# One hybrid decoder layer on one core: the place of the last norm's sums among the steps of a group

## What is computed

```python
proj = n1 @ w_in                                 # (320 x 2048) @ (2048 x ...)
xbc_c = silu(causal_dwconv(xbc, xbc0, ssm_conv_w, ssm_conv_b))     # B, C and x, 4 taps
xs, Bm, Cm = split_last(xbc_c, ...)
y, h_new = ssd_scan(xs_h, dt, A, Bm, Cm, ssm0)   # 8 groups of 8 heads
y = y + ssm_d[:, None] * xs_h
y = y * silu(z)
yg = y.reshape(b, L, 8, 512)                     # one norm for each group
yg = yg * rsqrt(mean(yg * yg, axis=-1) + EPS)
branch_a = (yg * ssm_norm) @ w_ssm_out
```

## Time and profile before

| | us |
|---|---|
| median of three runs | 2808.53 |
| lowest and highest | 2807.86, 2808.56 |
| the profiled execution's own time | 2808.5 |
| its span | 2806.8 |
| TensorE busy in the span | 2783.4 (99%) |
| VectorE busy | 1782.3 (63%) |
| ScalarE busy | 1165.9 (42%) |
| mean granted TensorE clock, share of full | 0.996 |

### The profile page before, as it was taken

One profiled execution on the slowest core, in us unless ns is written; L12 is line 12 of the kernel. 1 busy time (PEld: TensorE's weight loads), 2 busy tenths in 40 slices (PEclk: granted clock), 3 DMA queues, 4 the chain that ended last, 5 costly groups with the idle time before them and its releaser, 6 DMA issues.

```text
span 2806.8 us, 53359 instructions
## 1 busy us (share of the span) xinstructions
PE 2783.4 (99%) x19380; PEld 2753.6 (98%) x19380; DVE 1782.3 (63%) x2247; ACT 1165.9 (42%) x1712; POOL 294.5 (10%) x457
## 2 busy tenths in 40 slices
PE   8999999999999999999999999999999999999998
PEld 7999999999999999999999999999999999999998
DVE  8888878887888655545454556555555555555564
ACT  5654454544544333333333336333333333333453
POOL 2222221222222100000000001000000000000100
PEclk9999999999999999999999999999999999999999
DMA  8887887887878665555555554555555555555553
GB/s 227 223 213 193 213 229 187 199 219 197 215 194 210 187 178 149 155 145 147 150 150 150 149 149 133 166 150 146 149 149 149 149 149 149 149 149 149 151 166 113
DMA packets 910210, 477.18 MB, mean 170 GB/s; under 512 B 167802, under 2 KB 903746, under 8 KB 909778
## 3 DMA queue, kind: packets, MB, share of 16 engines
q1 hardware_dynamic: 833345, 433.15, 57.3%
q10 hardware_dynamic: 76080, 40.03, 5.2%
q0 software_dynamic: 672, 2.66, 0.2%
HBM read 449.95 MB, written 25.79 MB: 169 GB/s over the span
## 4 chain that ended last, share of the span: by engine, by line
PE 97%; DVE 1%; ACT 0%; issue 0%; DMA 0%; SPq 0%; ACTq 0%; DVEq 0%
PE ps L1842 31%; PE ps L1843 31%; PE ps L1844 31%; PE ps L2098 1%; PE ps L1950 1%; PE ps L2114 1%; PE ps L2016 0%; PE ps L2006 0%; PE ps L2007 0%; PE ps L2233 0%; PE ps L2240 0%; PE ps L2244 0%; DMA xrow<-in_x_sample 0%; PE ps L2105 0%; PE ps L2218 0%
## 5 line engine op out<-in xcount | busy, mean ns | idle before, releaser
L1842 PE MATMUL ps<-n_hi,whi 128*128 128x320 f32 x4144 | 1285.2, 310 | 0.8 <-DVE chunk L1573 0.6
L1844 PE MATMUL ps<-n_hi,wlo 128*128 128x320 f32 x4144 | 1280.6, 309 | 0.0
L1843 PE MATMUL ps<-n_lo,whi 128*128 128x320 f32 x4144 | 1280.5, 309 | 0.0
L1176 DVE TENSOR_TENSOR wlo<-raw,whi 128x1024 fp32r<-128x1024 f32 x746 | 922.2, 1248 | 462.7 <-ACT whi L782 461.9
L782 ACT ACTIVATE whi<-raw 128x1024 fp32r<-128x1024 f32 x746 | 783.3, 1057 | 833.6 <-PE ps L1844 722.1
L1842 PEld LDWEIGHTS ps<-n_hi,whi 128*128 128x128 f32 x4144 | 778.0, 188 | 3.6 <-DVE chunk L1573 0.9
L1843 PEld LDWEIGHTS ps<-n_lo,whi 128*128 128x128 f32 x4144 | 777.9, 188 | 1.3
L1844 PEld LDWEIGHTS ps<-n_hi,wlo 128*128 128x128 f32 x4144 | 777.8, 188 | 0.0
L1842 PE MATMUL ps<-c_hi,whi 128*128 128x320 f32 x1728 | 535.1, 310 | 0.5 <-DVE c_lo L1299 0.5
L1844 PE MATMUL ps<-c_hi,wlo 128*128 128x320 f32 x1728 | 533.9, 309 | 0.0
L1843 PE MATMUL ps<-c_lo,whi 128*128 128x320 f32 x1728 | 533.9, 309 | 0.0
(11 more groups left out here) (309 smaller groups left out, 1752.6 us busy)
## 6 DMA issues: line engine op xcount, KB each, us to landing
raw<-in_w_in SPq DMA_DIRECT2D x322, 512.0 KB, 4.6
raw<-in_w_ffn_gate SPq DMA_DIRECT2D x88, 512.0 KB, 4.6
raw<-in_w_ffn_up SPq DMA_DIRECT2D x88, 512.0 KB, 5.0
raw<-in_w_ffn_down SPq DMA_DIRECT2D x88, 512.0 KB, 4.0
raw<-in_w_ssm_out SPq DMA_DIRECT2D x64, 512.0 KB, 6.0
hs<-in_state_ssm ACTq DMA_DIRECT2D x32, 512.0 KB, 5.9
hq<-in_state_ssm SPq DMA_DIRECT2D x512, 32.0 KB, 3.3
out_ssm_sample<-hs ACTq DMA_DIRECT2D x32, 512.0 KB, 3.6
```

Of the source, the lines that this page charges most:

```text
L1176: tt(wlo[slot][:], raw[slot][:], whi[slot][:].bitcast(F32), SUB).then_inc(lo_split, 1)
L1842: mm(out, w_h, x_h, start=first, stop=False)
L1843: mm(out, w_h, x_l, start=False, stop=False)
L1844: return mm(out, w_l, x_h, start=False, stop=last)
```

## The change

In the list for groups 1 to 7 `norm` moves from behind the second unit to behind the fourth, directly ahead of `bc`, and `lows` moves from behind the third unit to behind `bc`. Nothing is added and nothing is removed; group 0, the short-convolution segment and all other segments keep their lists.

```diff
-        head = (x(0, 1) + [("norm", 0)] + x(2) + [("lows", 0)] + x(3) + [("bc", 0)] + x(4)
+        head = (x(0, 1) + x(2) + x(3) + [("norm", 0), ("bc", 0), ("lows", 0)] + x(4)
                 + OUT8[:1] + [("flip", 0)] + OUT8[1:3] + [("old", 0)] + OUT8[3:5] + [("decay", 0), ("clamp", 0)]
                 + OUT8[5:6] + [("exps", 0)] + OUT8[6:] + [("mask", 0)] + x(5))
```

## The result

| | before | after |
|---|---|---|
| median, us | 2808.55 | 2847.8 |
| lowest and highest | 2807.86, 2808.73 | 2847.5, 2849.72 |
| span of the profiled execution | 2806.8 | 2845.9 |
| mean granted TensorE clock | 0.996 | 0.991 |

The ratio is 1.0143, with a 95% interval of 1.0131 to 1.0155: the change makes the kernel 39.3 us slower. The forecast was 2833.8, and its range ended at 2846.0. The sign and the place were right, but the time lies 1.8 us outside the range.

The account below looks back on a forecast made before the run. TensorE was taken to bound the loop, with no idle time to absorb a wait. (3.52 + 0.1) x 7 = 25.3 us on 2808.5 gave 2833.8 us, +0.9%, with a range of 2829 to 2846.

Parts of the forecast that it names:

- What bounds the kernel: In the loop TensorE is busy 112.00 of 112.00 us a round, so any new wait adds to the time, seven-fold.
- Part 1: TensorE's own work at the norm's sums: same work in another order, gain taken as 0, at most 2.8 us.
- Part 2: First out step: the third c_lo tile comes at T + 12.53, TensorE is ready at T + 9.18; 3.52 us lost a round.
- Part 3: Third and sixth out steps: VectorE's later additions may delay TensorE by 0 to 1 us a round; 0.1 taken.
- The rival of the clock: TensorE's clock falls in the new gap: another 16 us, 2850 in all rounds, 2836 to 2848 in some; chance 0.15.
- The rival of a covered wait: c_lo arrives before the fifth unit ends, 2808.5 to 2811.7 us; bc behind lows would leave 0.45 us a round; chance 0.06.

Follow-up runs that it names:

- the kernel with other banks: Changed kernel with lows ahead of bc, the first out step writing banks 2 and 3, its b_stacked and cbm_ready waits one step later: 2832.3 us.
- the kernel with a gap of 3.8 us: Changed kernel with lows ahead of bc behind the fourth unit: 2850.6 us, ratio 1.0154 to the kernel before.

## Why the prediction was right and wrong, point by point

- **What bounds the kernel, and that a wait has no slack to go into.** Right. 7 waits, and no other engine's change shows in the loop. Only moving `lows` gave 0.9999, so the move of `norm` is what costs.
- **Part 1, nothing gained on TensorE.** Right: the sums take 0.53 us in their new place (162.48 to 163.01), and the turns behind them start as closely as before.
- **Part 2, the chain.** VectorE's side was right to the hundredth: T + 12.53 predicted, 174.86 - 162.33 = 12.53 measured. The order of the queue and every duration in it came from rows, so this was not luck. TensorE's side was T + 9.18 against 171.36 + 0.147 - 162.33 = 9.18. Mis-sized was the term from the tile's end to the start: 0.06 taken, 0.32 measured, so that the gap was 3.51 us and not 3.25. Most of the difference is the waits queued behind c_lo's, as the kernel with c_lo's wait last shows. With 3.76 to 3.80 us a round at full clock (8 and 24 matmuls in the gap) the forecast's 3.62 was 1.1 us short in all.
- **Part 3, the additions.** The range of 0 to 1 us held, at its lower end: no wait for `acc_a` in the changed kernel. There the slow matmuls gave VectorE more time: the first addition ends at 181.72, 2.1 us ahead of the third out step at 183.79. The reckoning itself is tested by the kernel with 24 matmuls, where the clock stays up. Its first addition ends at 181.16 and the third out step starts at 181.75, a lead of 0.6 where 0.3 was reckoned; its fourth ends at 191.98 and the sixth out step starts at 193.50, a lead of 1.5 where -0.3 was reckoned. So the 0.1 us in the sum stood for nothing. That the lead is thin is shown by the kernel with other banks, where TensorE came sooner and did wait 1.6 us for the addition.
- **The rival of the clock.** This is the step that failed: the sum has no term for the clock and takes TensorE's matmuls behind the gap at their full pace ("the clock stays at 1.00"). The fall was left to a rival. It was described with its mechanism and priced at 16 us for all rounds; it came in all of them and took 39.3 - 7 x 3.78 = 12.8 us, which the 108 slow matmuls (13.0 us) account for. It was given a chance of 0.15, on the reason that a single gap between two dense stretches has no like in the rows and need not do what a wait among transposes did. The runs show the opposite: one gap of 3.5 us in 117 sends the clock down each time, one of 2.3 us in two rounds of seven, one of 1.55 never. The Trainium skill's warning on idle gaps between bursts of matmuls ("TensorE: Matmul & The Clock Gate", section "HAM oscillation — how this bites in real kernels") agrees with the trace here for the gaps of 3.3 us and more; that they do so each time does not hold for 2.3 us. It deserved more weight than the absence of a row. Forecast and rival together, 2833.8 + 16 = 2850, would have been 2 us off, but in part by luck: the price of the fall was 3 us too high and the wait 1.1 us too low.
- **The rival of a covered wait.** Not what happened, and its reckoning was wrong as well: turning `bc` and `lows` round leaves no 0.45 us but a longer wait, since `b_stacked`, which the front part itself names, is asked for at the same place.
- **The range.** It took in half of the clock's case and so ended at 2846.0. With gaps of 3.3 to 3.8 us the clock fell in all 7 rounds of each of three kernels, so for the gap that was forecast half of the rival was a poor bound. It is not all or nothing at every length, as the 2.3 us show.

## What to carry to other kernels

When the bounding engine has no idle time, a moved step costs the difference between its chain to the consumer and the work left beside it; that can be added up from start-to-start times of the trace to a tenth of a microsecond, if everything queued ahead on each engine is counted, as well as each further wait of the consumer. A new idle gap on TensorE can cost more than its own length. In these kernels no gap in the loop of up to 1.6 us sent the clock down, one of 2.3 us did so in two rounds of seven, and one of 3.3 us or more always did: from there on take the slow matmuls behind it into the sum. A few matmuls in the gap are worth a try if it can't be closed. A wait that goes away mostly uncovers the next, as long as the late engine's queue is as long as before.

## What the runs showed of the hardware

- With a gap of 3.5 us in each round the granted clock fell from 1.00 to 0.50 in every round: in the first round at the restart, in the second 1.4 us ahead of it, in the gap. In the kernel with a gap of 3.8 us it also fell 1.2 us behind the restart.
- In the changed kernel it came back after 12 matmuls in one round and 20 in the next. The first such round costs 1.5 us and the other 2.4. The kernel with the gap of 3.8 us has no such turn.
- Eight matmuls whose result nobody uses made the changed kernel 10.5 us faster: with the gap at 2.33 us and not 3.51 the clock stayed up in five rounds of seven.
- Three further satisfied waits between a late one and the first matmul cost 0.18 us.
- A longer TensorE program brought stops without a releaser far behind the edited place, of 10.0, 4.7 and 3.0 us with 24, 16 and 32 more matmuls, and none with 8. That the place of the code in memory causes them is a guess that no run shows.
